# First layer's expert gate and up products: full 128x128 weight blocks as the stationary operand, instead of two 64-column halves

## The reference, cut to what matters

```
def ec_moe(h, w_router, w_e_gate, w_e_up, w_e_down):
    b, t, d = h.shape
    cap = EC_CAPACITY * t // N_EXPERTS          # 64 latent, 32 context tokens
    aff = jax.nn.softmax((h @ w_router).astype(jnp.float32), axis=-1)
    vals, idx = lax.top_k(jnp.swapaxes(aff, 1, 2), cap)
    xs = jax.vmap(lambda hb, ib: hb[ib])(h, idx)
    hid = jax.nn.silu(jnp.einsum('becd,edf->becf', xs, w_e_gate)) * jnp.einsum('becd,edf->becf', xs, w_e_up)
    ys = jnp.einsum('becf,efd->becd', hid, w_e_down) * vals[..., None].astype(h.dtype)
    ...
```

## Time and profile before

| | |
|---|---|
| median of three timed runs | 3601.54 us |
| profiled execution: device time | 3597.66 us |
| profiled execution: span of the trace | 3595.9 us |
| TensorE busy, share of the span | 3397.3 us, 94% |
| TensorE weight loads busy | 2343.4 us, 65% |
| VectorE, ScalarE busy | 1170.0 us, 707.2 us |
| first layer's expert stage | 1195.76 to 2000.57 us |
| read from HBM over the span | 706.15 MB |
| mean granted TensorE clock | 0.989 |

### The profile page before, as it was taken

One profiled execution on the slowest core, in us unless ns is written; L12 is line 12 of the kernel. 1 busy time (PEld: TensorE's weight loads), 2 busy tenths in 40 slices (PEclk: granted clock), 3 DMA queues, 4 the chain that ended last, 5 costly groups with the idle time before them and its releaser, 6 DMA issues.

```text
span 3595.9 us, 74576 instructions
## 1 busy us (share of the span) xinstructions
PE 3397.3 (94%) x32464; PEld 2343.4 (65%) x32464; DVE 1170.0 (33%) x2535; ACT 707.2 (20%) x1346; POOL 99.8 (3%) x171
## 2 busy tenths in 40 slices
PE   7899999999999999999999989899999999999998
PEld 4456757678764777777677656667677565555554
DVE  1443415336624211111111362415265242222222
ACT  3313321122322000000001432321132201111111
POOL 0000100000000000000000000100000000000000
PEclk9999999999999999999999999999999999999999
DMA  5512120020034999999999501220211269999995
GB/s 219 221 51 71 35 82 12 30 71 34 27 129 200 352 367 356 362 366 375 347 358 345 185 31 44 70 82 13 82 45 53 110 262 420 423 419 418 420 421 244
DMA packets 104784, 732.84 MB, mean 204 GB/s; under 512 B 8464, under 2 KB 14864, under 8 KB 61472
## 3 DMA queue, kind: packets, MB, share of 16 engines
q1 hardware_dynamic: 95120, 692.54, 48.7%
q0 software_dynamic: 9360, 35.71, 3.5%
HBM read 706.15 MB, written 16.83 MB: 201 GB/s over the span
## 4 chain that ended last, share of the span: by engine, by line
PE 78%; DMA 9%; DVE 7%; ACT 3%; issue 3%; DVEq 0%; POOL 0%; ACTq 0%; SPq 0%; POOLq 0%
PE psum L709 14%; PE psum L1308 10%; PE psum L1299 8%; PE psum L1337 8%; PE psum L599 8%; PE psum L592 5%; PE psum L1162 4%; PE psum L711 3%; DMA ring<-in_w_e_gate 3%; DMA ring<-in_w_ada 2%; DMA ring<-in_w_e_down 2%; PE psum L1343 2%; PE psum L1353 2%; PE psum L576 2%; DVE work L2045 2%
## 5 line engine op out<-in xcount | busy, mean ns | idle before, releaser
L709 PE MATMUL psum<-HT,ring 128*128 128x256 f32 x2560 | 599.3, 388 | 13.9 <-DVEq L2298 5.3
L709 PEld LDWEIGHTS psum<-HT,ring 128*128 128x128 f32 x2560 | 487.7, 194 | 97.8 <-issue 21.3
L1308 PE MATMUL psum<-work,ring 128*64 128x96 f32 x11264 | 486.4, 248 | 42.5 <-issue 33.1
L1308 PEld LDWEIGHTS psum<-work,ring 128*64 128x64 f32 x11264 | 473.0, 138 | 59.7 <-issue 49.7
L1528 ACT ACTIVATE work<-psum,small 128x768 f32<-128x768 f32 (+4 forms) x208 | 146.1, 703 | 682.7 <-PE psum L1343 323.1
L599 PE MATMUL psum<-ring,HT 128*128 128x512 f32 (+1 forms) x768 | 276.0, 521 | 0.0
L1337 PE MATMUL psum<-ring,work 128*64 128x512 f32 x1056 | 240.6, 597 | 6.4 <-DMA ring<-in_w_e_down 6.3
L1531 ACT ACTIVATE work<-psum 128x256 f32<-128x256 f32 (+7 forms) x219 | 103.5, 473 | 696.1 <-PE psum L1322 259.1
L599 PEld LDWEIGHTS psum<-ring,HT 128*128 128x128 f32 x768 | 145.8, 190 | 127.3 <-issue 120.5
L592 PE MATMUL psum<-HT,ring 128*128 128x256 f32 (+3 forms) x624 | 192.8, 470 | 0.3 <-issue 0.3
L1299 PE MATMUL psum<-ring,work 128*64 128x256 f32 x768 | 173.7, 381 | 0.0
(11 more groups left out here) (249 smaller groups left out, 4021.0 us busy)
## 6 DMA issues: line engine op xcount, KB each, us to landing
ring<-in_w_e_gate SPq DMA_DIRECT2D x48, 2048.0 KB, 10.8
ring<-in_w_e_up SPq DMA_DIRECT2D x48, 2048.0 KB, 11.4
ring<-in_w_e_down SPq DMA_DIRECT2D x48, 2048.0 KB, 10.2
ring<-in_w_ada SPq DMA_DIRECT2D x24, 2048.0 KB, 12.7
ring<-in_w_e_gate SPq DMA_DIRECT2D x24, 1536.0 KB, 9.4
ring<-in_w_e_up SPq DMA_DIRECT2D x24, 1536.0 KB, 9.6
ring<-in_w_e_down SPq DMA_DIRECT2D x24, 1536.0 KB, 10.2
ring<-in_w_gate SPq DMA_DIRECT2D x16, 2048.0 KB, 8.8
```

What stands on the lines that cost most here:

```text
L709: pe.matmul(b[:, 0:256], w[:, k, d4 * P:(d4 + 1) * P], HT[:, k, off:off + 256], start=(k == 0), stop=(k == KD - 1))
L1308: ins = pe.matmul(b[lo:lo + 64, f * cap:(f + 1) * cap], w[k][:, c0:c0 + 64], e_xs[:, k, 0:cap], start=(k == 0), stop=(k == KD - 1))
```

## The change

The two 64-column halves become one matmul with all 128 columns stationary and an output over all 128 partitions of the bank. The number of tokens that move, the banks, the semaphores and the order of the work stay.

```
@@ gate_up, first layer @@
 for k in range(KD):
-    for half in range(2):
-        lo, c0 = 64 * half, f * P + 64 * half
-        ins = pe.matmul(b[lo:lo + 64, f * cap:(f + 1) * cap], w[k][:, c0:c0 + 64], e_xs[:, k, 0:cap],
-                        start=(k == 0), stop=(k == KD - 1))
+    ins = pe.matmul(b[:, f * cap:(f + 1) * cap], w[k][:, f * P:(f + 1) * P], e_xs[:, k, 0:cap],
+                    start=(k == 0), stop=(k == KD - 1))
```

## The result

The changed kernel takes 3694.56 us (median of 4 runs, 3687.28 to 3700.51), the kernel before 3603.53 us in the same comparison: a ratio of 1.0254, 95% interval 1.0226 to 1.0281. It is slower by about 91 us. The forecast was 3704 us, +2.8%.

What follows compares the result with a forecast made beforehand. TensorE and DMA were taken as nearly level in the first expert stage. +163.5 us from loads, -60 of waits, +3 that stay: stage 911 us against 804.8, forecast 3704 us (+2.8%), range 3678 to 3732.

Steps and rivals of the forecast that it cites:

- What bounds it now: First expert stage, 804.8 us: TensorE and DMA nearly level, TensorE's own work 745 us, about 60 us waiting.
- my 46.3: First expert of the first expert stage: 46.3 us of TensorE time with next to no waiting, taken for all sixteen.
- my 4: Last expert of the stage: 4 us added to the sum for its other work in place of a choice of tokens.
- The halves cost 82.6 ns a pair and their loads are hidden: Gate and up before: two halves take 82.6 ns, set by streaming 96 columns; their side-by-side loads need about 60 ns.
- A full record is load-bound at 111.6 ns: Gate and up after: loading 128 stationary columns sets 111.6 ns a record, +163.5 us of TensorE time over 5632 records.
- The first rival: Gate and up: full loads hide under the matmul before, record 82.6 ns, stage -30 us, 3572 us; chance 10%.
- Waits are given back: First expert stage: the 60 us of waits go as TensorE work is added, 3 us of waits stay.
- Code pauses: 33.1 us of "issue" pauses before gate and up, read as TensorE waiting for code behind weight traffic; nearly gone after.
- a 4% rival: Loads don't overlap at all: record 190 ns, 4145 us; TensorE at half clock would end in the same region; chance 4%.

## Why the prediction was right, point by point

- *What bounds it now.* Two level resources, and some 60 us of waits. Right. With half the weight traffic the second expert takes 45.9 us (1242.26 to 1288.12), not my 46.3, so the waits were 67 us by that base: 804.8 - 16 x 45.9 - 3.3 for the last expert. (Its other work costs 3.3 us more than a choice; my 4 had a wait of 0.73 us in it.) Half the traffic gave back 59 of the 67.
- *The halves cost 82.6 ns a pair and their loads are hidden.* Right, and shown by the pair at 59 ns when less moves.
- *A full record is load-bound at 111.6 ns.* Measured 112.0 in a run. The added work, 16 x (56.16 - 45.9) = 164 us, was forecast as 163.5. The rows that gave it were two loads 0.11 us apart and a line with ordinary full loads. The first rival, that loads hide, fell with the pace itself; the run that moves 128 columns and the run that loads 96 say that the load sets it. The run with 64 columns moving says the same where the clock was full. The Trainium skill's figure of about 81 ns for a matmul of 128 moving columns (TensorE: Matmul & The Clock Gate, Back-to-back issue gap) is not what f32 blocks do here: with 128 moving, a record took 112 ns.
- *Waits are given back.* 60 us less 3 forecast; about 66 of 67 us came back. These were the mis-sized terms of the sum, and they put the stage at 902.5 us against 911. The forecast was built on the profiled execution before, and the profiled execution after, 3700.5 us, is only 3.5 us under it: the 8.5 us of the stage, less the 5.0 us of later start. The median is 5.9 us lower still. So part of the closeness is luck of the executions.
- *Code pauses.* Right: they stand every 256 instructions, end when a packet of code has landed, went from 33.1 to 0.7 us with half the code, and rose to 79.2 us when the same code ran quicker. That the fetch waits behind packets of weights is not shown; that it is slower under their load is.
- *What I missed.* The clock. I gave it part of a 4% rival. The forecast held, but on a margin I did not know: the same blocks with 64 columns moving lose half the clock.

## What to carry to other kernels

For f32 weights as the stationary operand, set the load of a record against its streaming: with 96 columns moving, a record with one load of 128 columns takes 112 ns, longer than the streaming (82.6 ns), while two loads of 64 into the two halves of the array run side by side (59 ns for the pair when little moves) and hide. Fewer, larger instructions are not cheaper as such. A stage with two level resources forgives added work up to its slack and then charges in full (0, 29 and 91 us here for a sixth of the pieces, half and all), so price a change there against each resource alone.

## What the runs showed of the hardware that was not expected

- Load-bound matmuls can lose the clock: full blocks with 64 columns moving ran at a granted clock of 0.50 in the long run of gate and up in 13 of 16 experts, 46.81 us for a run that takes 25.23 at full clock, though TensorE's rows show no pause. With 96 or 128 columns moving, at the same 112 ns a record, the stage's clock was 1.00.
- Code has to be fetched: at 29 ns a record TensorE paused 79.2 us in one 800 us stage for instructions. Together with a DMA that was already at 0.96 of the time, 130 us less of matmul work bought 6 us.
